# GpSimd adds pairs of C products, and PE multiplies the states with two sets instead of four

## The reference

```python
uf = u.astype(f32); ug = uf.reshape(bsz, seq, 64, 16)          # 64 groups of 16 channels
bu_re, bu_im = einsum('blgc,gpc->blgp', ug, b_re), einsum(..., b_im)
in_re, in_im = f_re * bu_re - f_im * bu_im, f_re * bu_im + f_im * bu_re
_, _, s_re, s_im = associative_scan(combine, (ab_re, ab_im, in_re, in_im), axis=1)   # 64 complex states
y = einsum('blgp,gcp->blgc', s_re, c_re) - einsum('blgp,gcp->blgc', s_im, c_im)
y = gelu(y.reshape(bsz, seq, 1024) + d_skip * uf)
y = y * sigmoid(y @ w_glu + b_glu)
```

## Time and profile before

| | |
|---|---|
| median of 3 runs | 1232.91 us |
| the profiled execution's own time | 1233.9 us |
| its span | 1232.1 us |
| PE busy | 1204.2 us (98%) |
| VectorE busy | 897.7 us (73%) |
| ScalarE busy | 638.7 us (52%) |
| GpSimd busy | 97.7 us (8%) |
| granted TensorE clock | 0.999 of full speed |

### The profile page before, as it was taken

The page is one execution under the profiler, slowest core; times in us unless marked ns, Lnnn a source line. Parts: engine busy times, 40 slices in busy tenths (PEclk is TensorE's granted clock), DMA queues, the critical chain, the costliest instruction groups (busy, mean ns, idle before and its releaser), DMA issues.

```text
span 1232.1 us, 19092 instructions
## 1 busy us (share of the span) xinstructions
PE 1204.2 (98%) x7597; PEld 1010.3 (82%) x7597; DVE 897.7 (73%) x1479; ACT 638.7 (52%) x1050; POOL 97.7 (8%) x163
## 2 busy tenths in 40 slices
PE   7999999999999999999999999999999999999998
PEld 3656778888988888787999987988788787999986
DVE  7888867767589998687656655589997687666553
ACT  4333565676546665545444544556575546444441
POOL 6200021101000200201000002000200201000000
PEclk9999999999999999999999999999999999999999
DMA  7735565434565455355656664564445355555551
GB/s 248 223 98 173 206 208 192 154 132 143 163 209 160 154 163 191 126 171 169 213 199 190 194 194 157 174 210 170 156 154 188 135 171 171 195 197 191 193 196 73
DMA packets 71959, 215.69 MB, mean 175 GB/s; under 512 B 16256, under 2 KB 19744, under 8 KB 71744
## 3 DMA queue, kind: packets, MB, share of 16 engines
q1 hardware_dynamic: 65008, 206.37, 50.6%
q0 software_dynamic: 2112, 6.97, 1.9%
q10 hardware_dynamic: 4752, 1.14, 0.4%
HBM read 208.95 MB, written 3.15 MB: 172 GB/s over the span
## 4 chain that ended last, share of the span: by engine, by line
PE 85%; DVE 7%; ACT 4%; issue 2%; POOL 1%; DMA 0%; SPq 0%; DVEq 0%; POOLq 0%; ACTq 0%
PE acc L704 17%; PE acc L706 17%; PE acc L705 17%; PE acc L682 7%; PE acc L683 7%; PE acc L684 7%; PE acc L643 4%; DVE weights_lo L1803 1%; PE mixed L1044 1%; PE mixed L1140 1%; ACT junk L1306 1%; DVE h_T L1833 1%; ACT weights_hi L1271 1%; PE mixed L1028 1%; PE turned L1094 1%
## 5 line engine op out<-in xcount | busy, mean ns | idle before, releaser
L1803 DVE TENSOR_TENSOR weights_lo<-weights_raw,weights_hi 128x1024 fp32r<-128x1024 f32 (+1 forms) x304 | 355.8, 1204 | 73.5 <-ACT weights_hi L1271 73.2
L1271 ACT ACTIVATE weights_hi<-weights_raw 128x1024 fp32r<-128x1024 f32 (+1 forms) x304 | 305.3, 1043 | 79.8 <-DMA weights_raw<-stream_dram 79.5
L704 PE MATMUL acc<-weights_hi,act_F_hi 128*128 128x512 f32 (+1 forms) x680 | 274.9, 404 | 5.4 <-DVE weights_lo L1803 3.2
L706 PE MATMUL acc<-weights_hi,act_F_lo 128*128 128x512 f32 (+1 forms) x680 | 266.0, 391 | 0.0
L705 PE MATMUL acc<-weights_lo,act_F_hi 128*128 128x512 f32 (+1 forms) x680 | 264.3, 389 | 0.0
L682 PE MATMUL acc<-act_F_hi,weights_hi 128*128 128x256 f32 x624 | 173.9, 279 | 0.0
L683 PE MATMUL acc<-act_F_hi,weights_lo 128*128 128x256 f32 x624 | 172.8, 277 | 0.0
L684 PE MATMUL acc<-act_F_lo,weights_hi 128*128 128x256 f32 x624 | 172.8, 277 | 0.0
L704 PEld LDWEIGHTS acc<-weights_hi,act_F_hi 128*128 128x128 f32 x680 | 128.0, 188 | 33.9 <-DVE weights_lo L1803 4.0
L706 PEld LDWEIGHTS acc<-weights_hi,act_F_lo 128*128 128x128 f32 x680 | 127.8, 188 | 28.1
L705 PEld LDWEIGHTS acc<-weights_lo,act_F_hi 128*128 128x128 f32 x680 | 128.0, 188 | 25.1
(11 more groups left out here) (343 smaller groups left out, 1920.2 us busy)
## 6 DMA issues: line engine op xcount, KB each, us to landing
weights_raw<-stream_dram SPq DMA_DIRECT2D x306, 512.0 KB, 3.7
weights_raw_more<-stream_dram SPq DMA_DIRECT2D x58, 512.0 KB, 3.9
gains<-rows_dram POOLq DMA_DIRECT2D x12, 512.0 KB, 4.9
weights_raw<-stream_dram SPq DMA_DIRECT2D x6, 416.0 KB, 3.0
weights_raw<-stream_dram SPq DMA_DIRECT2D x4, 384.0 KB, 3.5
x_T<-x_in_dram SPq DMA_DIRECT2D x4, 256.0 KB, 6.1
ssm_bc<-ssm_bc_dram SPq DMA_DIRECT2D x1, 1024.0 KB, 8.3
u_scratch<-u_T ACTq DMA_DIRECT2D x4, 256.0 KB, 4.7
```

What stands on the lines that cost most here:

```text
L704: pe.matmul(o, xh, wh, start=first and kk == 0, stop=False)
L706: i = pe.matmul(o, xl, wh, start=False, stop=last and kk == s["nk"] - 1)
L1271: act.activation(high(s, slice(0, n)), whole(s, slice(0, n)), ACT.Copy).then_inc(hi_made, 1)
L1803: dve.tensor_tensor(low(s, slice(0, n)), whole(s, slice(0, n)), high(s, slice(0, n)).bitcast(F32), ALU.subtract).then_inc(lo_made, 1)
```

## The change

VectorE still makes four products, in the order 0, 2, 1, 3, and raises `c_mats_made` after the third and after the fourth of them. GpSimd adds set 1 to set 0, and set 3 to set 2, in place, each one TENSOR_TENSOR of 128 x 1024, and raises `c_sums_made`. PE waits for both sums of a part and multiplies with sets 0 and 2 alone. The eight additions stand in GpSimd's queue between `load_gain(3)` and `load_gain(4)`.

```diff
@@ states_part, PE
                 pe.wait_ge(states_made, qd + 1)
-                pe.wait_ge(c_mats_made, qd + 1)
+                pe.wait_ge(c_sums_made, 2 * (qd + 1))
                 cm = (c_alt, c_mat)[qd % 2]
-                for n in range(4):
+                for n in (0, 2):
                     for q in (0, 2, 4, 6, 1, 3, 5, 7):
                         for e in range(2):
...
                             i = pe.matmul(o, st[rowsel, qd % 2, n // 2, q, :], cm[rowsel, n, q, :], start=False,
-                                          stop=(n == 3), skip_group_check=True)
-                            if q == PQ - 1 and n == 3:
+                                          stop=(n == 2), skip_group_check=True)
+                            if q == PQ - 1 and n == 2:
                                 i.then_inc(y_ready, 1)
@@ SP
-                        sp.wait_ge(c_mats_made, PARTS)
+                        sp.wait_ge(c_mats_made, 2 * PARTS)
@@ c_mats, VectorE
                 tt(o[0], pr, cr, ALU.mult).then_inc(dve_steps, count())
-                tt(o[1], pi, ci, ALU.mult).then_inc(dve_steps, count())
                 tt(o[2], pr, ci, ALU.mult).then_inc(dve_steps, count())
                 dve.wait_ge(dve_steps, count.n)
+                tt(o[1], pi, ci, ALU.mult).then_inc(c_mats_made, 1)
                 tt(o[3], mi, cr, ALU.mult).then_inc(c_mats_made, 1)
@@ GpSimd
             load_gain(2)
             load_gain(3)
+
+            for qd in range(PARTS):
+                cm = (c_alt, c_mat)[qd % 2]
+                for k in range(2):
+                    pool.wait_ge(c_mats_made, 2 * qd + k + 1)
+                    tt(cm[:, 2 * k, :, :], cm[:, 2 * k, :, :], cm[:, 2 * k + 1, :, :], ALU.add).then_inc(c_sums_made, 1)
+
             load_gain(4)
```

More of the change, by code:

```diff
@@ L423, in build @@
         c_mats_made = sem("c_mats_made")
+        c_sums_made = sem("c_sums_made")
         c_paired = sem("c_paired")
```

## The result

| | before | after |
|---|---|---|
| median of the executions | 1232.98 us (1232.85 to 1233.51, 4) | 1251.01 us (1248.66 to 1251.46, 4) |
| profiled execution | 1233.9 us | 1248.66 us |
| its span, mean granted clock | 1232.1 us, 0.999 | 1246.9 us, 0.989 |

The change makes the kernel slower: the ratio is 1.0139 [1.0127, 1.0151], 18.0 us by the medians. The two profiled executions differ by 14.8 us. The forecast of 1244.4 us had the sign and the place of the loss, but the time is above the end of its range, 1249.5.

The account below looks back on a forecast made before the run. PE and VectorE were taken to share the critical path; GpSimd's additions, less PE's savings, put the first GLU product at 122.6 instead of 111.06 us, +11.5. 1233.9 + 11.5 = 1245.4, less 1.0 to the median: 1244.4 us, range 1235.5 to 1249.5.

Parts of the forecast that it names:

- What bounds the kernel: PE and VectorE share the critical path; whatever slows VectorE between 39 and 105 us reaches PE.
- The hold of VectorE: VectorE's products with two SBUF inputs stand still behind each GpSimd addition, for its whole 2.25 us.
- parts 2 and 3: First addition beside the scan's PSUM products holds the rest by 0.85 us, the second by 2.25: 3.1 us a part.
- rival (d): All of VectorE's operations stand still behind additions, the PSUM ones too: +14.4 us, 1247.3 us; chance 0.12.
- Rival (a): The additions hide, not holding VectorE up: -2.1, 1230.8 us, up to -3.5, 1229.4 us; decided at b_mats(2); chance 0.15.
- (b): GpSimd is starved by back-to-back VectorE operations, so sums come late: +13 to +15, 1246 to 1248 us; chance 0.12.
- (c): An addition holds VectorE 1.10 us, as a copy: +2.6, 1235.5 us; chance 0.08 including cases up to the forecast.
- Part 0: Both additions start at 39.5 us beside b_mats(1); VectorE loses 4.5 us less about 0.1 of idle; PE +4.0 at taps(1).
- PE after its waits: PE, there at 69.4 us, waits over 6 us for taps(2) at 75.7 (+8.2), then goes on at old speed.
- The saving of PE: 64 of 128 instructions fewer per states_part, 1.0 us each; counted in parts 1 and 2, nothing in parts 0 and 3.

Follow-up runs that it names:

- e5: The changed kernel with PE kept at work in its waits for VectorE by turns (identity transposes that compute nothing used): 1245.78 us, ratio 1.0106.
- e7: e5 with one GpSimd addition a part instead of two, PE multiplying three sets, turns fitted to shorter waits: 1239.96 us, ratio 1.0068.
- the copies: e5 with GpSimd copies in place of the additions, two products missing from the output, turns fitted to shorter waits: 1237.7 us, ratio 1.0041.
- e12: e5 with the two additions of part 0 moved ahead of GpSimd's three gain loads: 1245.47 us, ratio 1.0099.
- e1: The kernel before, with PE multiplying sets 0 and 2 alone, no sums, products 1 and 3 left out of the output: 1237.51 us, ratio 1.0022.
- e3: The kernel before, with one added PE wait at taps(1) until part 0's states are made, no sums: 1241.96 us, ratio 1.0068.
- e11: e1 with turns on PE before the three taps and the first GLU product: 1231.08 us, ratio 0.9982 to the kernel before.
- e2: The changed kernel with 58, 46 and 14 turns on PE before taps(1), taps(2) and taps(3) only: 1248.85 us, ratio 1.0126.
- e8: The kernel before, with VectorE making part 1's sums in its idle time and PE multiplying two sets in that part: 1235.73 us, ratio 1.0018.
- e9: Control: the kernel before with nine turns on PE before taps(2): 1235.35 us, ratio 1.0019.
- e10: e8 with nine and fourteen turns on PE before taps(2) and taps(3): 1232.53 us, ratio 0.9998 to the kernel before.

## Why the prediction was right, and where it failed

The walk below goes by the starts of PE's steps. "Forecast" is the prediction's own sum, and "after" is the profiled execution.

| | before | forecast | after | e5 |
|---|---|---|---|---|
| `taps(1)` | 49.83 | 53.8 | 55.14 | 56.21 |
| `taps(2)` | 67.49 | 75.7 | 76.88 | 77.22 |
| `taps(3)` | 85.79 | 93.0 | 97.11 | 94.49 |
| first GLU product | 111.06 | 122.6 | 126.44 | 123.87 |

In e5 `taps(1)` is later than in after because the 58 turns before it run 0.8 us past the end of `b_mats(1)` at 55.45 us; VectorE does not wait for that.

**What bounds the kernel: right.** PE and VectorE share the critical path, and what holds VectorE reaches PE: each of PE's three long waits ends with `b_mats`.

**The hold of VectorE: right, as a mechanism and mostly in size.** An addition was taken at 2.25 us; the single one of e7 holds a product by 3.37 - 1.22 = 2.15. Two on `b_mats(2)` were to cost 4.4 us; they cost 2 x (3.37 - 1.22) = 4.3 in e5. In after it is 2.43 + 3.37 - 2.44 = 3.4, as VectorE first waited 0.88 us for PE's late turn of L875, and GpSimd added in that time. That `b_mats(2)` waits on PE there is a dependence that the forecast did not have; the time is the same, 3.36 + 0.88 = 4.24. In parts 2 and 3 the forecast had 3.1 us each: the rows give 3.62 - 0.76 = 2.9 and 0.12 for the products of c (3.61 against 3.49). The scan's products from PSUM ran unhindered at 1.41 us, and only the pair of SBUF products behind them was long.

That rules out rival (d), in which the PSUM products stand still too. The rule of the Trainium skill (SBUF — State Buffer, "Who interferes with whom") says the same of both: a VectorE instruction with two SBUF inputs contends with a GpSimd instruction that reads SBUF, and one with at most one SBUF input does not, outside the 2-port modes, a condition that the forecast left out. The trace agrees, with 3.37 us for the first kind and 1.41 for the second. Rival (a), in which the additions hide, falls with the 3.37 us, (b) with the additions having their turn after one VectorE operation at most, and (c) with the copies: these do hold for less, but an addition is no copy.

**Part 0: mis-sized.** The forecast gave both additions of part 0 "4.5 us less about 0.1 of idle", with one VectorE operation between them. They cost 5.75, and the first product of the pair stood through both. `taps(1)` is 1.3 us later than forecast for it and `taps(2)` 1.2. e12 shows that it is the place behind the DMA issues: there the VectorE operation that began at 38.20 stood until the additions were done, from before their own start at 39.43 (the times of GpSimd's records are rough). Ahead of the issues the hold is 4.13 us, and the first GLU product comes at 122.47, where the forecast had 122.6. Why the issues add 1.6 us was not taken further.

**The step that failed: PE after its waits.** The sum let PE go on at its old speed after "PE, which would be there at 69.4, waits over 6 us", and so had `taps(3)` 17.3 us after `taps(2)`. With the clock kept that is met, 94.49 - 77.22 = 17.27 in e5, though there VectorE's `b_mats(3)` alone sets it: the 1.48 us of `issue` are gone, PE is early, and 14 turns fill its wait. In after it is 97.11 - 76.88 = 20.23 us, 2.9 more. The way of it: `taps(2)` and what follows run at half clock, z comes late to VectorE (its wait before z at 88.70 is 6.20 us, in before 3.24), and `b_mats(3)` stands behind z. The fall at `taps(1)` is covered, since PE waits for `b_mats(2)` in any case, and so is the fall at `taps(3)`, behind which VectorE sets the time: from `taps(3)` to the GLU it is 29.33 us in after and 29.38 in e5, 29.6 in the forecast. Together: 1.2 for part 0, 2.9 for the clock, -0.3 for the last stretch, so 3.8 us over the forecast's 122.6. At the end of the kernel 14.8 of the 15.4 us by which the first GLU product is late are left.

The forecast noticed PE's waits and counted them as lost time alone. The trace of before could have raised the question, as it showed no PE wait over 1.48 us in this stretch, but it held no row that gives the price, and its one wait of 1.69 us, at 271.30, kept the clock; e1 and e3 do give the price.

**The saving of PE: smaller than priced.** It was taken at 1.0 us a part; 2.03 - 1.16 is 0.87. By itself it is worth some 2.2 us (e11), and -4 us with PE's waits left idle (e1), because the time it frees is spent in waits behind which the clock falls.

**The range: too narrow above.** Its end, 1249.5, had the bounds of the hold and none for a slower PE. With the 2.9 us of the clock and the 1.2 of part 0 the forecast would have been 1248.5, inside the range. The median is 2.5 us above that still, and nearly all of it is the 2.35 us between the profiled execution and the median, which no run explains.

**What stays open.** Three of four executions of after took 1250.72 to 1251.46 us, 2.1 to 2.8 more than the profiled one. A further fall of the clock, at the waits of 1.20 and 1.77 us before the GLU, would have that size. But one fall lowers the mean clock by some 0.003 (0.996 or 0.997 with one in e2 and e8, 0.994 with two in e1), and the three have 0.989, 0.989 and 0.988 beside the profiled one's 0.989, which speaks against it. Their cause stays open. The 0.9 us of before lie within its scatter (1231.52 to 1234.38 us in the ten runs beside e1). Nor is it settled what makes the `issue` times, or the single executions some 4 us over their median at full granted clock (e7's 1243.73, e9's 1240.38, e10's 1237.71). In the profiled one of e10, 4.1 us over its median, the last FFN's matmuls took longer, though the windows give the granted clock as 1.0. Groups of PE, 1070 to 1200 us, of before and then of e10:
```profile
L683 PE MATMUL acc<-act_F_hi,weights_lo 128*128 128x256 f32 x202 | 55.8, 276 | 0.0
```
```profile
L684 PE MATMUL acc<-act_F_hi,weights_lo 128*128 128x256 f32 x196 | 55.1, 281 | 0.0
```

## What to carry to other kernels

Before work is given to an idle GpSimd, ask what VectorE does meanwhile: beside its products of two SBUF inputs an addition of 128 x 1024 costs VectorE 2.15 us, whether GpSimd had time or not, and beside its products from PSUM nothing. Where a change makes PE wait, price the work behind the wait as well: here waits of 1.60 to 6.59 us before `taps` were followed by 6 to 8 us of PE's work at half clock, some 3 us lost, which behind the shorter waits is more than the wait itself. Waits of 1.69 and 1.77 us before GLU products cost nothing of the kind, so look at the granted clock behind each wait and not at its length alone. And an instruction saved on PE just ahead of a wait is no gain, and can be a loss.

## What was not expected of the hardware

- **A lighter PE was slower.** e1, with 64 matmul instructions a part left out and nothing added, took 1237.51 us beside 1233.51; with transposes of no use in its waits it took 1231.08 beside 1233.27.
- **The clock fell after waits as short as 1.60 and 1.61 us** (e1, e8), both before `taps`; after 1.13 us there, after 1.77 us before the GLU (after) and after 1.69 us at 271.30 (before) it did not. Between executions of e8 it sometimes fell and sometimes not, 3 us apart.
- **GpSimd's hold of VectorE began before its addition did, behind DMA issues:** 5.75 us for two additions right behind three loads, 4.13 us for the same two ahead of them. The loads without additions, in before, held nothing.
- **PE's unexplained idle times move with its code:** the 1.48 us before 79.43 are gone in after and in e1, with 64 instructions less a part, and in e9, with 9 turns more, there are three, of 0.58, 1.52 and 0.75 us. Another, of 0.73 us ahead of the L905 at 95.66 in before, is in all four.
